# Two products at once: the scores of two heads side by side in a forgetting attention, and the pairwise decay sums of a chunked scan as two fp32r products over four heads

## What is computed

```python
# scan: 32 heads in 4 groups, chunks of 128 rows
adt = dt * a; a_cs = cumsum(adt)                    # within a chunk
decay[l, s] = exp(a_cs[l] - a_cs[s])  for s <= l, else 0
y_diag = (C B^T * decay) @ (x * dt)                 # beside it a state carried from chunk to chunk
# attention: 16 heads of 64
c = cumsum(logf)
s[t, j] = q_t . k_j / 8 + c[t] - c[j]   for j <= t, else -inf
out = softmax(s) @ v
```

## Time and profile before

| | |
|---|---|
| three runs | 2472.65, 2472.85, 2477.55 us |
| the profiled execution | 2477.41 us, of which the span of its instructions is 2475.3 us |
| mean granted TensorE clock | 0.994 of full speed |
| scan, 1580 to 2016 us of the span | 436 us |
| attention, 2016 to 2326 us | 310 us |

### The profile page before, as it was taken

How to read it: one execution, slowest core, us unless ns; L and a number is a source line. 1 busy time by engine, 2 the same in 40 slices (tenths; PEclk the granted TensorE clock), 3 DMA queues, 4 the chain that set the end, 5 groups by cost and what they waited for, 6 DMA issues and landing times.

```text
span 2475.3 us, 34710 instructions
## 1 busy us (share of the span) xinstructions
PE 2404.4 (97%) x14354; PEld 2009.5 (81%) x14354; DVE 1298.8 (52%) x2101; ACT 879.4 (36%) x1499; POOL 374.9 (15%) x301
## 2 busy tenths in 40 slices
PE   8999999999999999999999999999999999999999
PEld 6778888888887777656888887988989878877788
DVE  3775625543535776875333336366565445554433
ACT  4331211111224444444222224364545333444422
POOL 0210000000014444501000001143343410000000
PEclk9999999999999999999999999999999999999999
DMA  9834334434321111012333332221222121121222
GB/s 324 204 94 125 119 103 130 126 119 118 104 68 35 52 38 48 35 44 76 92 96 102 95 93 86 69 69 52 69 69 78 60 69 52 52 69 52 77 94 111
DMA packets 252744, 220.79 MB, mean 89 GB/s; under 512 B 7480, under 2 KB 243443, under 8 KB 252204
## 3 DMA queue, kind: packets, MB, share of 16 engines
q1 hardware_dynamic: 249072, 217.92, 28.7%
q10 hardware_dynamic: 3260, 0.58, 0.1%
q0 software_dynamic: 256, 0.07, 0.0%
HBM read 214.26 MB, written 6.29 MB: 89 GB/s over the span
## 4 chain that ended last, share of the span: by engine, by line
PE 59%; ACT 3%; DVE 3%; issue 2%; POOL 1%; DVEq 0%; ACTq 0%; POOLq 0%
PE two L685 10%; PE bank L1354 5%; PE bank L1545 4%; PE bank L685 4%; PE bank L1350 3%; PE bank L1331 3%; PE two L1285 3%; PE bank L1526 2%; PE bank L1051 2%; PE two L1156 2%; PE bank L1182 2%; PE two L1565 2%; PE bank L1021 1%; PE bank L1033 1%; PE two L1297 1%
## 5 line engine op out<-in xcount | busy, mean ns | idle before, releaser
L2568 DVE TENSOR_TENSOR wL<-ring,wH 128x512 fp32r<-128x512 f32 x224 | 182.5, 829 | 225.3 <-ACT wH L1840 225.1
L1831 ACT ACTIVATE wH<-ring 128x2048 fp32r<-128x2048 f32 (+1 forms) x80 | 149.1, 1864 | 272.4 <-PE bank L690 73.4
L2557 DVE TENSOR_TENSOR wL<-ring,wH 128x2048 fp32r<-128x2048 f32 (+1 forms) x80 | 180.4, 2255 | 82.2 <-ACT wH L1831 82.0
L685 PE MATMUL two<-h1H,wH 128*128 128x512 f32 x496 | 195.5, 394 | 0.0
L685 PE MATMUL two<-h1H,wL 128*128 128x512 f32 x496 | 193.4, 390 | 0.0
L685 PE MATMUL two<-h1L,wH 128*128 128x512 f32 x496 | 193.3, 390 | 0.0
L1840 ACT ACTIVATE wH<-ring 128x512 fp32r<-128x512 f32 x224 | 133.6, 623 | 58.8 <-PE bank L1331 21.1
L1909 ACT ACTIVATE gateS<-two 128x512 f32<-128x512 f32 x44 | 26.3, 598 | 332.2 <-PE bank L690 142.0
L2661 DVE SCALAR_TENSOR_TENSOR xT<-two,ada,xT 128x512 f32<-128x512 f32 (+1 forms) x48 | 30.6, 679 | 186.2 <-PE bank L690 66.3
L3204 POOL TENSOR_TENSOR rstd<-rstd,sq 128x768 f32<-128x768 f32 (+1 forms) x15 | 30.4, 2024 | 611.4 <-ACT sq L1867 610.2
L1354 PE MATMUL bank<-unH,wH 128*128 128x272 f32 (+1 forms) x368 | 112.2, 305 | 3.9 <-ACT cin L2100 2.1
(11 more groups left out here) (642 smaller groups left out, 6953.5 us busy)
## 6 DMA issues: line engine op xcount, KB each, us to landing
ring<-in_ffn_w_in SPq DMA_DIRECT2D x88, 512.0 KB, 5.1
ring<-in_w_in SPq DMA_DIRECT2D x40, 1024.0 KB, 5.0
ring<-in_w_ada SPq DMA_DIRECT2D x32, 1024.0 KB, 5.2
ring<-in_ffn_w_out SPq DMA_DIRECT2D x16, 1024.0 KB, 5.1
early<-in_w_ada SPq DMA_DIRECT2D x12, 1024.0 KB, 12.0
ring<-in_diff_w_in SPq DMA_DIRECT2D x12, 1024.0 KB, 5.2
ring<-in_w_proj_ssd SPq DMA_DIRECT2D x8, 1024.0 KB, 4.9
ring<-in_ffn_w_out SPq DMA_DIRECT2D x8, 768.0 KB, 4.5
```

The costliest lines, as they stand in the source:

```text
L685: m = nc.tensor.matmul(bank[3 * s + half], w, r[:, 0:LAT], start=i == 0, stop=i == n - 1)
L1831: nc.scalar.activation(hi, raw, ACT.Copy).then_inc(w_hi, 1)
L2557: nc.vector.tensor_tensor(lo, raw, hi.bitcast(F32), ALU.subtract).then_inc(w_lo, 1)
L2568: nc.vector.tensor_tensor(lo, raw, hi.bitcast(F32), ALU.subtract).then_inc(q_lo, 1)
```

## The change

Attention: q and k of two heads stay on 128 partitions (scaled by -1/8, so that scores come out negated), and `fox_scores(v)` makes both heads of a pair v = u // 2, head 0 from partitions 0 to 63 into `two[0]`, head 1 from 64 to 127 into `two[1]`. The query sums are dropped (they cancel in the softmax). The key sums go by one DMA to DRAM and from there by one DMA for every 8 units, broadcast to 128 partitions (`ckB`, two buffers); `fox_max` adds them in a `tensor_tensor_reduce` that also takes the minimum. The four loops run over 32 pairs instead of 64 units, probabilities have four buffers instead of two, and for i = 2 the turned meta columns go to free columns of bank 4 and are copied by ScalarE. Scan: GpSimd builds `useg` in two passes (adt rounded to fp32r, then the rest) times the upper triangle, and `segments` multiplies the fp32r lower triangle, stationary, by 4 heads at a time: 2 products of 512 columns for each pass, added in PSUM. Some small tiles are laid out elsewhere.

```diff
@@ TensorE, segments(n)
-                pe.wait_ge(p_lseg, n + 1)
+                pe.wait_ge(p_lseg, 2 * n + 1)
...
-                for h in range(8):
-                    m = nc.tensor.matmul(two[0][:, h * P:(h + 1) * P], lseg[:, h * P:(h + 1) * P], upper, start=True, stop=True)
+                for x in range(2):
+                    if x:
+                        pe.wait_ge(p_lseg, 2 * n + 2)
+                    for h in range(0, 8, 4):
+                        m = nc.tensor.matmul(two[0][:, h * P:(h + 4) * P], lowerR[:], useg[:, x, h:h + 4, :].rearrange("p h s -> p (h s)"),
+                                             start=x == 0, stop=x == 1)
@@ TensorE, fox_scores(v), f, p, i = v // 8, v // 4 % 2, v % 4
-                if u >= 2:
-                    pe.wait_ge(b_exp, u - 1)
+                if v:
+                    pe.wait_ge(b_exp, 2 * v)
                     if i == 3:
-                        pe.wait_ge(b_ptd, u - 1)
-                n = META + (i + 1) * P
+                        pe.wait_ge(b_ptd, turned_apart(2 * v - 2))
                 for a, b in spans(i):
-                    m = nc.tensor.matmul(S[:, a:b], q[0:DH + 2, h, i * P:(i + 1) * P], k[0:DH + 2, h, a:b], start=True, stop=True)
-                m.then_inc(b_s, 1)
+                    for c in range(2):
+                        r = slice(DH * c, DH * c + DH)
+                        m = nc.tensor.matmul(two[c][:, a:b], q[r, p, i * P:(i + 1) * P], k[r, p, a:b], start=True, stop=True)
+                        if b == META + (i + 1) * P:
+                            m.then_inc(b_s, 1)
@@ TensorE, the loop (turned_apart(u): how many of the first u units VectorE copies)
-            for u in range(64):
-                if u < 63:
-                    fox_scores(u + 1)
-                next(beside)
-                fox_turn(u)
-                next(beside)
-                if u and u % 2 == 0:
-                    fox_out(u - 2)
+            for v in range(32):
+                if v:
+                    if v < 31:
+                        fox_scores(v + 1)
+                    next(beside)
+                    fox_turn(2 * v)
+                    next(beside)
+                    fox_out(2 * v - 2)
+                else:
+                    next(beside)
+                    next(beside)
+                    fox_scores(1)
+                    fox_turn(0)
+                next(beside)
+                fox_turn(2 * v + 1)
+                if v:
+                    next(beside)
+            next(beside)
@@ ScalarE, the loop (keys_act: one copy of 128 partitions instead of two of 64; at (-1, 23) one copy adt to adtR)
+            fox_exp(1)
+            for v in range(32):
+                m, r = v // 2, 2 * (v % 2)
+                split_hi_part(S_OF[UNITS[m]] + 1, r)
+                if v < 31:
+                    fox_exp(2 * v + 2)
+                    fox_exp(2 * v + 3)
+                if v % 4 == 1 and v > 4:
+                    fox_hi(v // 4 - 1)
+                fox_kept(2 * v)
+                if v % 2:
+                    first_act(UNITS[m])
+                elif v:
+                    second_act(UNITS[m - 1])
+                split_hi_part(S_OF[UNITS[m]] + 1, r + 1)
+                fox_kept(2 * v + 1)
@@ VectorE, fox_max and the loop
-                nc.vector.tensor_reduce(amx[:, u % 2:u % 2 + 1], two[u % 2][:, 0:n], AX.X, ALU.max, negate=True).then_inc(b_max, 1)
+                nc.vector.tensor_tensor_reduce(two[u % 2][:, 0:n], two[u % 2][:, 0:n], ckB[w % 2][:, u % 2, 0:n], 1.0, 3.0e38,
+                                               ALU.add, ALU.min, amx[:, u % 2:u % 2 + 1]).then_inc(b_max, 1)
...
+            for v in range(32):
+                m, r = v // 2, 2 * (v % 2)
+                if v < 31:
+                    fox_max(2 * v + 2)
+                    fox_max(2 * v + 3)
+                if v % 2:
+                    first_dve(UNITS[m])
+                elif v:
+                    second_dve(UNITS[m - 1])
+                split_lo_part(S_OF[UNITS[m]] + 1, r)
...
+            dve.wait_ge(x_out, 16)                                   # right after adt
+            link(nc.vector.tensor_copy(lowerR[:], lower))
@@ GpSimd, decays(i) and the DMAs
-                    nc.gpsimd.tensor_tensor(lseg[:, 0:8 * P].rearrange("p (h s) -> p h s", h=8), wide(adt[:, i, hs], P, P),
-                                            lower.unsqueeze(1).broadcast_to([P, 8, P]), ALU.mult).then_inc(p_lseg, 1)
+                    for x in range(2):
+                        nc.gpsimd.tensor_tensor(useg[:, x], wide(adtR[:, x, i, hs].bitcast(F32), P, P),
+                                                upper.unsqueeze(1).broadcast_to([P, 8, P]), ALU.mult).then_inc(p_lseg, 1)
...
-                nc.gpsimd.memset(qA[0][DH:DH + 2, :, :], 1.0).then_inc(b_one, 1)
-                nc.gpsimd.memset(kA[0][DH:DH + 2, :, :], 1.0).then_inc(b_one, 1)
...
+                pool.dma_start(decays_d, ckT[:, :]).then_inc(b_ck[0], 16)
...
+            for w in range(2, 8):
+                pool.wait_ge(b_max, 8 * w - 8)
+                if w % 2:
+                    pool.wait_ge(b_ck[w // 2], 16)
+                decays_in(w)
```

More of the change, by code:

```diff
@@ L320, in bass_two_blocks_kernel @@
         zrow = sb("zrow", [P, 4, 512])
-        dtt = sb("dtt", [P, 4 * 240])
-        dta, dtu, dtw, dtl = (dtt[:, 240 * k:240 * k + 240].rearrange("p (a n) -> p a n", a=5) for k in range(4))
-        ysq = dtt[:, 0:512]
-        expa = sb("expa", [P, 32])
-        logf = sb("logf", [P, 5, 16])
+        ysq = sb("ysq", [P, 512])[:]
         phase()
@@ L331, in bass_two_blocks_kernel @@
         wd = (sb("wdH", [P, KC, 48], F32R), sb("wdL", [P, KC, 48], F32R))
+        early_x = sb("early_x", [P, 1768])
+        dtt = sb("dtt", [P, 4 * 240])
+        dta, dtu, dtw, dtl = (dtt[:, 240 * k:240 * k + 240].rearrange("p (a n) -> p a n", a=5) for k in range(4))
+        expa = sb("expa", [P, 32])
+        logf = sb("logf", [P, 5, 16])
+        dtr = sb("dtr", [P, 5, 48])
+        adt = sb("adt", [P, 5, 32])
         leave()
@@ L554, in bass_two_blocks_kernel, with meta_turned @@
         UNITS = sum(BESIDE, [])
+        def meta_turned(u):
+            return bank[4][0:META, 3 * P:4 * P] if u // 2 % 4 == 2 else two[u % 2][0:META, 640:640 + P]
         WO = T_OF[("wo", 0)] % 2
@@ L1573, in fox_turn @@
                 if u >= 2:
-                    pe.wait_ge(b_ptd, u - 1)
+                    pe.wait_ge(b_ptd, turned_apart(u - 1))
                 for j in range(i + 1):
-                    nc.tensor.transpose(bank[4][:, j * P:(j + 1) * P], probA[:, u % 2, META + j * P:META + (j + 1) * P], ident)
-                nc.tensor.transpose(two[u % 2][0:META, 640:640 + P], probA[:, u % 2, 0:META], ident).then_inc(b_pt, 1)
+                    nc.tensor.transpose(bank[4][:, j * P:(j + 1) * P], probA[:, u % 4, META + j * P:META + (j + 1) * P], ident)
+                nc.tensor.transpose(meta_turned(u), probA[:, u % 4, 0:META], ident).then_inc(b_pt, 1)
             def fox_out(u):
@@ L2307, in _ @@
                 if (g, t) == (-1, 23):
+                    act.wait_ge(d_adt, 1)
+                    act.wait_ge(x_out, 16)
+                    nc.scalar.activation(adtR[:, 0], adt[:], ACT.Copy).then_inc(d_adt, 1)
                     act.wait_ge(d_sums, 1)
@@ L2337, in _ @@
             fox_exp(0)
-            for u in range(64):
-                m, r = u // 4, u % 4
-                if r == 0 and m:
-                    second_act(UNITS[m - 1])
-                if r == 2:
-                    first_act(UNITS[m])
-                if u < 63:
-                    fox_exp(u + 1)
-                if u % 8 == 1 and u > 8:
-                    fox_hi(u // 8 - 1)
-                split_hi_part(S_OF[UNITS[m]] + 1, r)
-                fox_kept(u)
+            fox_exp(1)
[11 more added lines that the diff above has]
+                elif v:
+                    second_act(UNITS[m - 1])
+                split_hi_part(S_OF[UNITS[m]] + 1, r + 1)
+                fox_kept(2 * v + 1)
             second_act(("gs", 2))
@@ L3027, in keys_dve @@
             def keys_dve(f, j):
-                for h in range(2):
-                    m = nc.vector.tensor_copy(kA[f % 2][0:DH, 2 * j + h, LO:ALL], bank[7][DH * h:DH * h + DH, 0:256])
-                    if h == 0:
-                        link(m)
-                m.then_inc(nB_free, 1)
+                nc.vector.tensor_copy(kA[f % 2][:, j, LO:ALL], bank[7][:, 0:256]).then_inc(nB_free, 1)
             def first_dve(key):
@@ L3111, in _ @@
                     scan_lo(q, o)
+                if (g, t) == (-1, 23):
+                    dve.wait_ge(d_adt, 2)
+                    link.wait()
+                    nc.vector.tensor_tensor(adtR[:, 1], adt[:], adtR[:, 0].bitcast(F32), ALU.subtract).then_inc(d_adt, 1)
                 if (g, t) == (3, 11):
```

145 lines of the change are left out of this document (74 added, 71 removed).

## The result

The changed kernel takes 2480.29 us, median of 11 runs (2478.26 to 2484.22). The kernel before, run beside it, takes 2473.58 us, median of 11 (2471.43 to 2477.55). The ratio is 1.0025 with a 95% interval of 1.0018 to 1.0033. So the change makes the kernel 6.7 us slower, where 2459.5 us and a gain of 13 were forecast. The profiled execution has a span of 2478.5 us against 2475.3, and a mean granted clock of 0.991 against 0.994.

What follows compares the result with a forecast made beforehand. TensorE was taken to bound both the scan and the attention. Scan -12, scores -25.3 and new waits +24 gave -13.3 us, from 2472.85 to 2459.5 us; range 2436 to 2472, the forecast's own 2452 to 2467.

Steps and rivals of the forecast that it cites:

- scan, decay sums on TensorE: Scan: cheaper fp32r products save 0.84 us per chunk step, counted for 14 of 16, 11.8 us.
- scores, with the waits for the meta copy: Attention: paired scores cost 28.6 us in place of 53.9, including 10.2 of waits for the meta copy: 25.3 us less.
- new waits for ScalarE: Attention: TensorE waits for ScalarE's later bank copies, 7.7 us for each of three f, some 24 us in all.
- Scan, GpSimd's part: Scan: second pass of 2.87 us or less per chunk step ends just in time at one place; that loss vanishes.
- Under half busy: Scan: GpSimd, busy 163 of 436 us, stays under half busy with 46 us more.
- The three bank waits: Attention: TensorE waits 2.2 us at keys' fifth chunk, 3.1 at keys to values, 2.4 at values to next unit.
- small bank waits: Rival, attention: ScalarE gets through its queue in time, so the scores' gain stands, 2438 us; chance 0.27.
- the second: Rival, attention: 64-row halves of a score pair do not overlap, 2478 us; chance 0.09 together with other trouble.
- Late throughout: Rival, scan: GpSimd's second pass is always late, so the decay sums save nothing, 2472 us; chance 0.16.

Runs made afterwards that it cites:

- the one-pass one: Changed kernel with GpSimd making only the first of its two passes, low part of the decays left out (timing only): 2465.08 us, ratio 0.9968.
- the attention alone: Changed kernel with the scan's decay sums put back as in the kernel before, attention left as changed: 2476.09 us, ratio 1.0010.
- the held-back pass: Changed kernel with GpSimd's second pass, for the first decay sums of the last three head groups, waiting for VectorE's split: 2471.29 us, ratio 0.9994.
- ScalarE's copies first: Changed kernel with ScalarE's copies of k and v units out of the banks ahead of its splits and exponentials: 2452.51 us, ratio 0.9918.

## Why the prediction was wrong

The profiled executions give the account. What one half-clock stretch costs comes from four kernels that run the same instructions in the attention with the same waits: the changed one and the one-pass one have four stretches there and take 319.54 and 319.62 us; the attention alone and the held-back pass have five, 321.18 and 321.18. So 1.6 us each. The scan agrees: with ScalarE's copies first it has the same waits as after and two stretches for three, and takes 433.25 us for 434.91.

| step | forecast, us | measured, us |
|---|---|---|
| scan, decay sums on TensorE | -12 | -11.5 (one pass, 420.00 less its one stretch, against the attention alone, 429.87, none) |
| scan, from the attention's part | 0 | -2.0 (429.87 against 433.47 less its one stretch) |
| scan, GpSimd's second pass | 0 | +11.7 (434.91 - 420.00, less two more stretches) |
| scan, clock | 0 | +3.2 (three stretches for one) |
| scores, with the waits for the meta copy | -25.3 | -21.4 (294.08 against 315.49) |
| new waits for ScalarE | +24 | +19.1 (319.54 - 294.08, less four stretches) |
| attention, clock | 0 | +6.4 (four for none) |
| ahead of the scan, the end | 0 | -2.25 |
| sum | -13.3 | +3.2 |

The medians differ by 6.7 and not by 3.2, since the profiled execution of before (2477.41 us) lies 3.8 us above the median of its runs and that of after on it (the two profiled times differ by 2.9, the spans by 3.2). The table accounts for these two executions; that the clock's term is no accident of theirs is shown by the mean clocks of all runs above: 0.991 for 0.995 is about 10 us of 2478, an estimate, and the table has 9.6.

**The step that failed is "Scan, GpSimd's part".** It asked who waits for the pass and found one place, the third chunk of the first group. That place was right: TensorE waits 1.54 us for `useg` there and nowhere else. It did not ask which instructions run beside the pass. "Under half busy" was taken as room; but a weight split of VectorE that ran beside the pass took 1.50 or 2.25 us instead of 0.69, and with the second pass more of them meet one. In the two lists of waits, after and with one pass, TensorE waits 4.6 us longer for the splits at L1361 (8.1 for 3.5), 2.9 for those at L1365 (3.1 for 0.2), 1.5 for `useg` and 1.3 for `cin` (3.1 for 1.8): 10.3 of the 11.7. The cause is shown by taking the pass away (split 0.69 us, 11.7 us back), by moving three of 32 (9.0 us back, 4.6 of them the three waits, the rest their stretches) and by adding it to the kernel before (13.8 us lost, 10.0 of them in the profiled scan). The Trainium skill (SBUF — State Buffer, section "SBUF: two separate sides") says that VectorE and GpSimd share a pair of ports by an exclusive lock, and that a VectorE instruction with two SBUF inputs and a GpSimd instruction that reads SBUF block each other for a whole instruction. The trace agrees: 2.25 us beside the pass, with the end 0.55 us after the pass has ended, and 0.69 us without it.

The pass's lateness in the third chunk was to vanish in the wait for ScalarE's copy `cin`, and the 1.54 us did. What did not vanish there came by VectorE again. Its timeline in the kernel after, beside the two passes of that chunk:

```profile
1615.15 3.67 DVE L2607 TENSOR_TENSOR wL<-ring,wH 128x512 fp32r<-128x512 f32 x2 [0.93 <-ACT wH L1870]
```

With one pass these two splits take 1.98 us (at 1612.00). Behind them VectorE makes `yrow`, for which GpSimd waits; for GpSimd's result waits ScalarE's norm, and behind that norm stands the copy into `cin`. Counted from the first decay sums, the product that waits for `cin` starts at 47.14 us in the kernel after and at 45.44 with one pass: 1.70 us later, and the two splits are 1.69 us longer.

**The second thing missing was the clock.** The prediction costed each wait of 2 to 3 us at its length. In the attention four of nine such waits (1.8 to 2.5 us) also brought a half-clock stretch, and so did the three of 2.7 us in the scan; less the one of the kernel before that is 9.6 us, more than the whole loss. That the waits bring the stretches is shown by the run that fills them with useless products: no stretch is left in the attention. The kernel before already showed one, behind its 1.91 us wait for `kA`, in a stage where the windows' clock column reads 1.00 because it is a mean over 436 us.

**What held.** The decay sums' saving (-12, -11.5). The scores: pairs overlap, priced at 3.57 us and measured at 3.53 in sum, in which there is luck: three of the four are 0.06 to 0.09 us dearer than priced and the one of 528 keys is 0.27 cheaper. The gain is still 3.9 us smaller than forecast. The rows show most of it: the prediction took the price of a single head up to the second product behind it and that of a pair only up to the first. Read like the single heads, the four pairs cost 3.93 us instead of 3.57, and 8 x 0.36 = 2.9 us. The remaining 1.0 us stays open. The three bank waits are at the places forecast, three times each and none in the last quarter, but 1.8, 2.5 and 1.9 us instead of 2.2, 3.1 and 2.4: 18.5 in place of 23, oversized by a fifth. Without the clock the attention would be 2.3 us faster than before (-21.4 + 19.1) where -1.3 was forecast; two errors of 4 and 5 us cancel there, which is luck too.

The rivals: small bank waits did not occur by themselves, though reordering ScalarE makes the first rival true for the attention. The halves overlap, so the second is out. "Late throughout" gave about the right size for the scan for the wrong reason, since the pass itself was late once only.

## What to carry to other kernels

When work is given to GpSimd, list what VectorE does in the same microseconds, and look at the instruction among them for which TensorE waits; a pass delayed by a microsecond was worth three here. Price a wait of TensorE like those here (1.8 to 2.7 us) above its length (about half of them cost 1.6 us more), and look for its clock in windows of 2 us, not in the stage's mean. And when an operation is merged, see what its engine's queue now holds ahead of the copies that free a bank: here moving the copies of the k and v units to the head of ScalarE's queue was worth twice the whole forecast gain.

## What the runs showed of the hardware

- A VectorE subtraction of 128x512 elements with both inputs in SBUF takes 0.69 us alone and 2.25 or 1.50 beside GpSimd's pass. The convolution's first step, one SBUF tensor by a column, takes 0.48 us alone and 2.12 beside it (at 1739.05 in the kernel with the held-back pass). GpSimd's pass is not steady either: 1.89, 2.34 or 2.88 us in the kernel after, for the same shape; which of VectorE's instructions lengthens it I did not trace.
- Seven half-clock stretches of the changed kernel follow waits of 1.8 to 2.7 us; in other kernels here one follows a wait of 1.58 us. Which waits have one differs between kernels with the same waits there: four of the attention's nine in two profiles, five in two others; of the three of 2.7 us in the scan all three in the kernel after, two with ScalarE's copies first. The 256-column products start 0.21 us apart in a stretch and 0.12 outside it. With the wait filled by useless products none follows.
- The product directly behind fp32 scores keeps TensorE longer: 0.31 us to the next start behind a single head of 528 keys, 0.33 or 0.34 behind a pair, 0.234 otherwise.
- One stretch more or less on the path is 1.6 us, which is part of the scatter between executions of one kernel (5 to 11 us between the fastest and the slowest of 11 or more runs).
